# Two transformer blocks, 256 tokens: dilated attention regrouped by pairs of heads, with values stationary

## What is computed

```python
def banded_window_attention(q, k, v, steps):      # per residue class of a group
    ...
    scores = jnp.where(valid, einsum(q, k) * HEAD_DIM ** -0.5, -inf)
    m = jnp.max(scores, axis=-1, keepdims=True)
    p = jnp.exp(scores - m)
    den = jnp.sum(p, axis=-1, keepdims=True)
    out = einsum(p / den, v)
    lse = m + jnp.log(den)

# DILATED_GROUPS = ((128, 1), (512, 4), (2048, 16)), 4 heads of 64 in each
alpha = jax.nn.softmax(jnp.stack(lses, axis=-1), axis=-1)
mixed = jnp.einsum('bshg,bshgd->bshd', alpha, o_all)
```

## Time and profile before

| | |
|---|---|
| Median of three runs | 707.49 us (707.36 to 707.54) |
| The profiled execution | 708.1 us |
| Its span, first to last instruction | 706.3 us |
| Busy: PE / weight loads / DVE / ACT | 697.0 / 615.3 / 492.2 / 400.1 us |
| Mean granted TensorE clock | 0.998 |
| HBM read | 122.36 MB, 175 GB/s over the span |

### The profile page before, as it was taken

How to read it: one execution, slowest core, us unless ns; L and a number is a source line. 1 busy time by engine, 2 the same in 40 slices (tenths; PEclk the granted TensorE clock), 3 DMA queues, 4 the chain that set the end, 5 groups by cost and what they waited for, 6 DMA issues and landing times.

```text
span 706.3 us, 10194 instructions
## 1 busy us (share of the span) xinstructions
PE 697.0 (99%) x4200; PEld 615.3 (87%) x4200; DVE 492.2 (70%) x669; ACT 400.1 (57%) x496; POOL 9.4 (1%) x25
## 2 busy tenths in 40 slices
PE   8999999999999999999999999999999999999996
PEld 7789999888888888888888998899988888888885
DVE  5875676979887766666545377677779878886452
ACT  6875855655555554555555555565547666664341
POOL 1000000003000000000000000000000000000000
PEclk9999999999999999999999999999999999999999
DMA  8863324655565555546551335454555545554511
GB/s 315 314 239 120 120 69 171 216 181 194 190 210 179 179 188 196 211 142 218 179 176 63 120 128 193 158 186 173 179 187 201 186 177 182 189 195 169 214 60 59
DMA packets 19341, 124.06 MB, mean 176 GB/s; under 512 B 2272, under 2 KB 2656, under 8 KB 5088
## 3 DMA queue, kind: packets, MB, share of 16 engines
q1 hardware_dynamic: 18144, 120.20, 48.1%
q10 hardware_dynamic: 1152, 3.22, 1.3%
HBM read 122.36 MB, written 1.05 MB: 175 GB/s over the span
## 4 chain that ended last, share of the span: by engine, by line
PE 89%; DVE 3%; ACT 3%; issue 2%; DMA 1%; SPq 1%; DVEq 0%; ACTq 0%
PE psum L1538 33%; PE psum L1539 17%; PE psum L1531 11%; PE psum L1533 11%; PE psum L1532 11%; PE psum L1527 2%; ACT whi L506 2%; DVE wlo L942 1%; DMA raw<-in_stream 1%; PE psum L1987 1%; PE psum L1950 1%; SPq L412 1%; PE psum L1949 0%; PE psum L2020 0%; DVE gates L1450 0%
## 5 line engine op out<-in xcount | busy, mean ns | idle before, releaser
L942 DVE TENSOR_TENSOR wlo<-raw,whi 128x2048 fp32r<-128x2048 f32 x110 | 251.8, 2291 | 92.6 <-ACT whi L506 92.6
L506 ACT CAST whi<-raw 128x2048 fp32r<-128x2048 f32 x110 | 209.5, 1907 | 49.8 <-PE psum L1533 44.1
L1538 PE MATMUL psum<-hx,whi 128*128 128x512 f32 x480 | 167.4, 393 | 0.0
L1539 PE MATMUL psum<-hx,wlo 128*128 128x256 f32 x480 | 134.4, 280 | 0.0
L1538 PE MATMUL psum<-yx,whi 128*128 128x512 f32 x352 | 125.3, 400 | 0.4 <-DVE yx L953 0.4
L1538 PEld LDWEIGHTS psum<-hx,whi 128*128 128x128 f32 x480 | 89.8, 187 | 19.8
L1539 PE MATMUL psum<-yx,wlo 128*128 128x256 f32 x352 | 98.8, 281 | 0.0
L1539 PEld LDWEIGHTS psum<-hx,wlo 128*128 128x128 f32 x480 | 90.7, 189 | 0.0
L1538 PEld LDWEIGHTS psum<-yx,whi 128*128 128x128 f32 x352 | 66.1, 188 | 16.9 <-DVE yx L953 0.9
L1539 PEld LDWEIGHTS psum<-yx,wlo 128*128 128x128 f32 x352 | 66.5, 189 | 0.0
L1531 PE MATMUL psum<-whi,hx 128*128 128x512 f32 (+1 forms) x160 | 62.5, 390 | 0.9 <-DVE wlo L948 0.7
(11 more groups left out here) (266 smaller groups left out, 1117.4 us busy)
## 6 DMA issues: line engine op xcount, KB each, us to landing
raw<-in_stream SPq DMA_DIRECT2D x110, 1024.0 KB, 4.8
raw<-in_stream SPq DMA_DIRECT2D x8, 256.0 KB, 6.0
relb<-in_relb ACTq DMA_DIRECT2D x1, 1536.0 KB, 7.8
x<-in_xT SPq DMA_DIRECT2D x4, 256.0 KB, 5.7
raw<-in_stream SPq DMA_DIRECT2D x2, 512.0 KB, 8.2
out_t<-sq SPq DMA_DIRECT2D x2, 320.0 KB, 2.7
final_gain<-in_final_gain ACTq DMA_DIRECT2D x1, 512.0 KB, 3.5
bsp<-in_bsp ACTq DMA_DIRECT2D x1, 384.0 KB, 3.3
```

The source lines that it names most:

```text
L506: act.copy(whi[s][:], raw[s][:]).then_inc(unit_hi, 1)
L942: dve.tensor_tensor(wlo[s][:], raw[s][:], whi[s][:], ALU.subtract).then_inc(unit_lo, 1)
L1538: pe.matmul(bank[b][:], stat[0], mov, start=first, stop=False, skip_group_check=True)
L1539: return pe.matmul(bank[b][:, 0:T], stat[1], mov[:, 0, :], start=False, stop=last, skip_group_check=True)
```

## The change

Scores are made by group instead of by head: `scores2(g)` does all four heads of group g, inside units 3, 5 and 7, each right after the group's q and k are transposed. The heads of a pair alternate. DVE adds the masks of group g (`max2(g)`) into a larger S2 that holds all heads; after the third group it takes the maxima. ACT exponentiates two heads each at units 8 and 9, DVE scales the probabilities by the reciprocal sums (`norm2`), PE turns 18 blocks per pair of heads after units 9 and 10 into banks 2 to 6, ACT copies them at units 10 and 11, and after units 10 and 11 PE multiplies with V stationary (64 columns) and the probabilities streaming. The result is feature-major, its halves are made from bank 7, and O2 and its transposes are gone. gate0, gate1 and gu2 become "f" units. `stats` issues a single matmul for n of 1 and above, and DVE adds the last tile. Buffers and banks are laid out anew (mask_sb, mi, mj, PT2, rtmp move).

```diff
-JOBS2 += [(f"gate{j}", "n" if j < 2 else "f", (19 + j if j < 4 else 11 + j,)) for j in range(8)]
-JOBS2 += [(f"gu{j}", "f" if j < 2 else "n", (j,)) for j in range(3)]
+JOBS2 += [(f"gate{j}", "f", (19 + j if j < 4 else 11 + j,)) for j in range(8)]
+JOBS2 += [(f"gu{j}", "f", (j,)) for j in range(3)]
...
-BANKS2.update({"gate0": (0,), "gate1": (1,), "gu2": (0,)})
-BANKS2.update({name: ((0, 1), (3, 7))[i % 2] for i, name in enumerate(n for n, kind, _ in JOBS2 if kind == "f")})
-WB_BANKS = (2, 3, 1, 0)
+BANKS2.update({name: ((0, 1), (2, 3))[i % 2] for i, name in enumerate(n for n, kind, _ in JOBS2 if kind == "f")})
+WB_BANKS = (2, 3, 0, 1)
...
+for _g in range(NG):
+    for _h in range(HG):
+        PLAN[4 + _h].append(("s2", _g, _h))
+for _r in range(HG // 2):
+    for _i in range(PT_BANKS):
+        PLAN[2 + _i].append(("pt2", _r, _i))
+    PLAN[7].append(("o2", _r))
...
-        S2 = sb("S2", [P, NG, 3 * P], scope=sa)
-        PT2 = sb("PT2", [P, NG, 3 * P], scope=sa)
+        S2 = sb("S2", [P, HG, NG, 3 * P], scope=sa)
...
+            def exp2(h):
+                if h == 0:
+                    act.wait_ge(s2_max, 1)
+                for t in range(TT):
+                    c = slice(0, P) if t == 0 else slice(P, 3 * P)
+                    ins = act.activation(S2[:, h, :, c], S2[:, h, :, c], ACT.Exp, bias=small[:, 64 + 2 * h + t:65 + 2 * h + t],
+                                         accum_out=small[:, 80 + 2 * h + t:81 + 2 * h + t])
+                ins.then_inc(s2_exp, 1)
+
+            def evac_pt2(r):
+
+                if r:
+                    full(act, 7, ("o2", 0))
+                for i in range(PT_BANKS):
+                    w = min(4 * P, (PT_BLOCKS - 4 * i) * P)
+                    full(act, 2 + i, ("pt2", r, i))
+                    act.copy(PT2[:, 4 * P * i:4 * P * i + w], bank[2 + i][:, 0:w]).then_inc(psum_free[2 + i], 1)
+
+            def yb_high(r):
+                full(act, 7, ("o2", r))
+                act.copy(yh[:, 6 + r, :], bank[7][:, r * T:(r + 1) * T]).then_inc(yb_hi, 1)

...
+                if n in (11, 12):
+                    yb_high(n - 11)
...
+                if n in (8, 9):
+                    exp2(2 * n - 16)
+                    exp2(2 * n - 15)
+                if n in (10, 11):
+                    evac_pt2(n - 10)
...
+                    if n == 22:
+                        u_gelu(0)
+                        u_gelu(1)
                     side_half(name, 1)
...
-                dve.tensor_tensor(sq[:, 0:2, :], sq[:, 0:2, :], sq[:, 4:6, :], ALU.add).then_inc(folded, 1)
+                ins = dve.tensor_tensor(sq[:, 0:2, :], sq[:, 0:2, :], sq[:, 4:6, :], ALU.add)
+                if n == 0:
+                    ins.then_inc(folded, 1)
+                else:
+                    done(ins)
+                    dve.tensor_tensor(sq[:, 0, :], sq[:, 0, :], sq[:, 1, :], ALU.add).then_inc(folded, 1)
...
-                if f == KT - 2:
+                if f == KT - 1:
...
+                    if f == KT - 1:
+                        gather(squares0, f)
...
+            def max2(g):
+
+                if g == 0:
+                    dve.wait_ge(masks2_done, 1)
+                for h in range(HG):
+                    full(dve, 4 + h, ("s2", g, h))
+                    for t in range(TT):
+                        c, m = slice(0, P) if t == 0 else slice(P, 3 * P), 6 * h + 3 * t + g
+                        ins = dve.tensor_tensor_reduce(S2[:, h, g, c], bank[4 + h][:, c], mask2[:, g, c], 1.0, -3e38,
+                                                       ALU.add, ALU.max, small[:, m:m + 1])
+                    ins.then_inc(psum_free[4 + h], 1)
+                if g == NG - 1:
+                    for h in range(HG):
+                        freed(dve, 4 + h, ("s2", g, h))
+                    dve.tensor_reduce(small[:, 64:64 + 2 * HG],
+                                      small[:, 0:2 * HG * NG].rearrange("p (q g) -> p q g", g=NG), AX.X, ALU.max,
+                                      negate=True).then_inc(s2_max, 1)
+
...
+            def norm2(r):
+
+                dve.wait_ge(s2_exp, 2 * r + 2)
+                d = small[:, 80 + 4 * r:84 + 4 * r]
+                done(dve.reciprocal(d, d))
+                for h in (2 * r, 2 * r + 1):
                     for t in range(TT):
                         c = slice(0, P) if t == 0 else slice(P, 3 * P)
-                        ins = dve.tensor_tensor_reduce(S2[:, g, c], bank[4 + g][:, c], mask2[:, g, c], 1.0, -3e38,
-                                                       ALU.add, ALU.max, small[:, 3 * t + g:3 * t + g + 1])
-                    ins.then_inc(psum_free[4 + g], 1)
-                for g in range(NG):
-                    freed(dve, 4 + g, ("s2", h, g))
-                dve.tensor_reduce(small[:, 64 + 2 * h:66 + 2 * h],
-                                  small[:, 0:3 * TT].rearrange("p (t g) -> p t g", t=TT), AX.X, ALU.max, negate=True)\
-                   .then_inc(s2_max, 1)
+                        ins = dve.tensor_scalar(S2[:, h, :, c], S2[:, h, :, c], small[:, 80 + 2 * h + t:81 + 2 * h + t], None,
+                                                ALU.mult)
+                    ins.then_inc(p2_normed, 1)
+
+            def yb_low(r):
+                dve.wait_ge(yb_hi, r + 1)
+                dve.tensor_tensor(yl[:, 6 + r, :], bank[7][:, r * T:(r + 1) * T], yh[:, 6 + r, :], ALU.subtract)\
+                   .then_inc(psum_free[7], 1)

...
+                if n in (11, 12):
+                    yb_low(n - 11)
...
+                if n in (9, 10):
+                    norm2(n - 9)
                 split(U_IN2 + n + 2)
+                if n in (3, 5, 7):
+                    max2((n - 3) // 2)
...
+            gather(16, KT - 1)
...
-                b, last = STATS_BANK[n], 1 if n < 2 else KT - 1
+                b = STATS_BANK[n]
                 free(pe, b, ("stats", n))
                 pe.wait_ge(folded, n + 1)
-                pe.matmul(bank[b][:, 0:T], ones[:], sq[:, 0, :], start=True, stop=False)
-                pe.wait_ge(squares, (4, 8, 16, 24)[n])
-                pe.matmul(bank[b][:, 0:T], ones[:], sq[:, last, :], start=False, stop=True).then_inc(psum_full[b], 1)
+                tiles_ = (0, 1) if n == 0 else (0,)
+                for i in tiles_:
+                    ins = pe.matmul(bank[b][:, 0:T], ones[:], sq[:, i, :], start=i == 0, stop=i == tiles_[-1])
+                ins.then_inc(psum_full[b], 1)

             def turn_b(j):
...
+                if u - U_IN2 in (3, 5, 7):
+                    scores2((u - U_IN2 - 3) // 2)
...
+            def turn_p2(r):
+
+                pe.wait_ge(p2_normed, 2 * r + 2)
+                for i in range(PT_BLOCKS):
+                    b, h, g, j = 2 + i // 4, 2 * r + i // 9, i % 9 // 3, i % 3
+                    if i % 4 == 0:
+                        free(pe, b, ("pt2", r, i // 4))
+                    ins = transpose(bank[b][:, i % 4 * P:(i % 4 + 1) * P], S2[:, h, g, j * P:(j + 1) * P])
+                    if i % 4 == 3 or i == PT_BLOCKS - 1:
+                        ins.then_inc(psum_full[b], 1)
+
+            def scores2(g):
+
+                freed(pe, 2, ("tq", g))
+                freed(pe, 3, ("tk", g))
+                for r in range(HG // 2):
+                    for t in range(TT):
+                        for h in (2 * r, 2 * r + 1):
+                            rows, b = slice(HD * (h % 2), HD * (h % 2) + HD), 4 + h
+                            if t == 0:
+                                free(pe, b, ("s2", g, h))
+                                pe.matmul(bank[b][:, 0:P], qT2[rows, g, r, 0:P], kT2[rows, g, r, 0:P], start=True, stop=True)
+                            else:
+                                pe.matmul(bank[b][:, P:3 * P], qT2[rows, g, r, P:T], kT2[rows, g, r, :], start=True,
+                                          stop=True).then_inc(psum_full[b], 1)
+
+            def values2(r):
+
+                for i in range(PT_BANKS):
+                    freed(pe, 2 + i, ("pt2", r, i))
+                free(pe, 7, ("o2", r))
                 for g in range(NG):
-                    if h == 0:
-                        freed(pe, 2, ("tq", g))
-                        freed(pe, 3, ("tk", g))
-                    free(pe, 4 + g, ("s2", h, g))
-                    pe.matmul(bank[4 + g][:, 0:P], qT2[rows, g, r, 0:P], kT2[rows, g, r, 0:P], start=True, stop=True)
-                    pe.matmul(bank[4 + g][:, P:3 * P], qT2[rows, g, r, P:T], kT2[rows, g, r, :], start=True,
-                              stop=True).then_inc(psum_full[4 + g], 1)
-
+                    for s in range(TT):
+                        for i in range(2):
+                            h, rows, at = 2 * r + i, slice(HD * i, HD * (i + 1)), (9 * i + 3 * g + 2 * s) * P
+                            ins = pe.matmul(bank[7][rows, r * T + s * P:(r + 1) * T], v2[:, s, g * UF + h * HD:g * UF + (h + 1) * HD],
```

(9 more changed lines are left out.)

138 lines of the change are left out of this document (22 added, 116 removed).

## The result

The changed kernel takes 699.18 us (median of four runs, 698.63 to 699.51) beside 707.51 for the kernel before on the same chip (707.36 to 708.19): ratio 0.988, 95% interval 0.9863 to 0.9897. On another chip, later, it was 699.24 (698.78 to 699.84) beside 708.54: 0.9873, 0.9858 to 0.9887. The forecast was 698.0, a ratio of 0.9866, with a range of 694.9 to 701.9, which holds both medians. The profiled execution took 698.63 us, its span is 696.7. Of the experiment "One ones-matmul, in the kernel before" two of eleven executions took 854.18 (the profiled one) and 980.53 us, at mean granted clocks of 0.753 and 0.655; they are left out of its ratio, and no row is read from that profile.

The account below looks back on a forecast made before the run. PE's queue was taken to set the time. Gains of 8.1 (attention), 1.3 (square sums) and 0.6 (units), less losses of 0.1 and 0.4, made 9.5: 707.5 - 9.5 = 698.0 us, range 694.9 to 701.9.

Parts of the forecast that it names:

- Scores, 5.1: Attention scores on PE: alternating heads overlap in different row halves, 1.7 us per group, 5.1 for three; gain 4.3.
- Values, 4.6: Probabilities times V on PE: two heads' passes run together, 2.3 us per pair of heads, twice 4.6; gain 3.2.
- the rival without overlap: Values on PE: the two heads' passes don't run together, +3.9 us, 701.9 in total; chance 0.07.
- Attention in all, 8.1: Scores, transposes and values in PE's queue: 21.8 us before, 13.7 after, a gain of 8.1.
- Square sums, 1.3: Three of four normalisations drop one of two ones-matmuls, 0.43 us each: gain 1.3, DVE's added sum hidden in the first two.
- Three units, 0.6: gate0, gate1, gu2: steps of 512 and 256 columns replace three of 256, 0.347 us for 0.360; gain 0.6, side work hidden.
- Loss at the start of FF2, 0.1: Last normalisation: DVE closes the addition with a wait ahead of the low half PE stands at; loss 0.1 us.
- (a): Scores in mid-unit wait for ACT's kT copy: nothing if the copy keeps its place, bound 0.1 us each.
- (b): Exponentials need all three groups; DVE's scalings end 9.3 us after unit 7, PE needs them at 10.9: slack 1.6.
- (c): ACT's copies of v and vg free bank 0 late for PE's unit 10: loss 0.4 us, between 0 and 1.5.
- rival (D): 18 transposes in a row beside thin passes drop the granted clock to 1.2 GHz; slower than before; chance 0.02.
- The cadence: Pairs of 512 and 256 columns keep 0.347 or 0.353 us in FF1 and FF2; left unchanged, 2.1 us either side.

Follow-up runs that it names:

- One ones-matmul, in the kernel before: Kernel before, with the second fold of square sums on VectorE and one ones-matmul instead of two at the three later statistics: 707.29 us beside 708.08, ratio 0.9987.
- mending: Changed kernel with VectorE's making of the second block's normalisation columns ahead of its bf16 split instead of behind it: 698.73 us, ratio 0.9866.

## Why the prediction was right, step by step

*What bounds the kernel.* Right: every saving that reached the time was one in PE's stream.

*Scores, 5.1.* Measured 3 x 1.71 = 5.1. The rows of the first block were the right ones to take the price from, and the alternation is what makes it.

*Transposes, 4.0.* Measured 2.06 for the first turn with entering and leaving, 1.94 for the second, which follows the values directly.

*Values, 4.6.* Measured 2 x 2.30, with 24 passes in 2.10. The reading of the gating's rows (eight double passes and two changes of shape) gave the figure to a tenth, by some luck: the passes took 2.10 for 2.0 forecast, the changes of shape 0.20 for 0.35. The price set for the rival without overlap, 8.5 in all, was too high, since in line a pair's passes took 3.45. The rule that was weighed against it, the Trainium skill's "TensorE: Matmul & The Clock Gate", Part 3 ("The mechanism"), that a weight load overlaps only where its row group differs, is not borne out: all these loads use all rows, and the 24 passes take 0.0875 us each with their loads. The Trainium skill's "TensorEngine Tiling (Array Packing)", "Key Properties", has it that different tiles can load and multiply in parallel; there the trace agrees (2.10 us with neighbours in different column halves, 3.45 without).

*Transposing O, 0.4.* The four transposes took 0.36 (416.48 to 416.84) and some 0.1 around them. The prediction counted them as time alone; the pairs behind them ran at the quick pace, and without them those of gate3 to gate5 are 0.3 slower.

*Attention in all, 8.1.* From the first turn of q and k to the gating PE's time fell by 8.26 (107.65 to 99.39). The gates' part of that is -0.3 and +0.2, so attention itself gave 8.35, some 0.3 more than forecast.

*Square sums, 1.3.* The matmuls went (0.43 three times), the gain did not all follow: one 0.43 came back as the wait at unit 2 (0.47 there for 0.07 before). The step that failed is "in the first two of them PE asks for it a unit or more later, so it is hidden". That was said of DVE's added sum and was true of it; what it left out is the next reader down the chain, ACT's copy of unit 0, which PE met with 0.07 us of delay already in the kernel before (its step there is 0.30 instead of 0.23). The last part gained twice what was forecast, 0.43 and another 0.4 by the pace.

*Three units, 0.6.* Mis-sized: the two gates gave 0.2 instead of 0.4, and gu2's 0.2 was taken back at FF2's start, so that the time shows next to nothing. The step that failed there is "beside units of 5.5 us", which put gu2's side copies and sums at nothing: they delay the chain to FF2's input by 0.3. The price of the new form had been read in FF1, at 0.347, though the prediction itself says that the pair has two cadences and FF2 shows the other.

*Loss at the start of FF2, 0.1.* The waits there grew by 0.37 (from 0.80 to 1.17 beyond the steps). 0.3 of this is the first wait, which gu2's form made. What the named mechanism is worth is the rest: the second wait grew by less than 0.1, and with the additions as before the stretch from the gating on is 0.05 shorter.

*(a)* No wait, as forecast. *(b)* The scalings end at 369.85, the turn starts at 371.16: 1.3 of room for 1.6 forecast, and scaling twice turned it into a wait. *(c)* Didn't come. ACT's and DVE's timelines of the changed kernel:

```profile
367.67 2.18 DVE L1385 TENSOR_SCALAR S<-S,small 128x384 f32<-128x384 f32 x4
...
364.27 0.62 ACT L824 ACTIVATE S<-S,small 128x384 f32<-128x384 f32 x1
...
372.18 0.46 ACT L883 ACTIVATE v<-psum,rcol 128x256 f32<-128x256 f32 x1
372.53 0.46 ACT L884 ACTIVATE vg<-psum,rcol 128x256 f32<-128x256 f32 x1
```

A head takes ACT 1.53 (364.27 to 367.32 for two, where the next cast starts) and not 1.63, and a copy 0.36. The copies are through the bank at 372.99 and PE wants it at 373.14. It was a loss of 0.4 put on a difference of two sums of some 13 us; the sign was not in reach.

*The clock, rival (D).* The granted clock was 1.00, the upper level of 2.4 GHz, through both turns and both blocks of values (start to end of a stretch, PE busy, then the clock behind the engines):

```profile
368.00:372.00 4.00, 4.00 (x23) 3.40 (x22) 4.00 (x5) 4.00 (x8) 0.00 (x0) 1.00 0.37 156
...
378.00:384.00 6.00, 6.00 (x51) 4.83 (x50) 1.24 (x2) 3.03 (x4) 0.00 (x0) 1.00 0.48 175
```

From 388 to 392 it was 1.00 too. Values and transposes followed each other for 4.0 us (378.76 to 382.80) with no dip. The Trainium skill's rule behind this rival ("TensorE: Matmul & The Clock Gate", Part 4: transposes don't count as activity) is not seen at work in these rows; no run here shows more.

*The cadence* was left as it was, with 2.1 us on either side. It flipped in three places: in FF2 for 23 us, which gave 0.4, in gate3 to gate5, which cost 0.3, and in the 16 pairs ahead of the fourth statistics, which cost 0.1. That these nearly cancel is luck. Besides, it was 0.353 in the two new gates, where the sum had 0.347.

*The bounds.* Two figures don't come out of their terms: 698.0 - 2.1 is 695.9, not 695.3, and less the 0.4 of (c) it is 695.5, not 694.9. (By its own terms the sum with exposed loads is 700.5, not 700.4.) Nothing hangs on either.

Where the 1.0 us of the attention stretch went, then: 0.4 at unit 2 (shown by undoing and by mending, which gave 0.5 and 0.6), 0.2 by the pace of the two new gate units (read in the trace, and found again when they were made narrow), 0.3 by the pace of gate3 to gate5 (read in the traces), 0.3 at FF2's start by gu2's form (shown by undoing it) and 0.1 by the pace behind that wait; less the 0.3 that attention gave beyond its forecast.

## What to carry to other kernels

When work is taken out of the engine that sets the time, look one unit further on for the reader it nearly met before: here a delay of 0.07 us in the old trace is where the saving stopped. Work added to an engine with room (gu2's sums on DVE, 71% busy) costs time where a chain to PE runs through it. Matmuls with 64 rows or 64 stationary columns should alternate between the two halves; one changed loop order cost 2.2 and 2.8 us here. And before moving an operation out of the way of an awaited one, see whether it fills a wait: then it costs nothing where it is.

## What the runs showed of the hardware

The alternating pair of a 512-column and a 256-column matmul has two paces, 0.347 and 0.353 us, at the same granted clock (1.00) and with the same operands, and keeps one until something else is issued or PE waits. In FF2 one ones-matmul ahead led to the quick one and two led to the slow one, in all thirteen profiles read here; four transposes ended the quick one wherever they stood (525, 537 and 581 us; sixteen in the first of these). Neither is a rule: in FF1 two ones-matmuls led to the quick one as well, and in the kernel before four transposes (at 416.48) ended a slow one. The spatial gating ended a slow one too (0.353 from 410.09, 0.347 from 430.00 on). Behind the second wait of FF2's start the same instructions ran 16 pairs at 0.347 in some kernels (the kernel before, the one with scores at the unit's end) and at 0.353 in others (the changed one). What inside PE fixes the pace is not known; no run tried it.

Two heads' scores in different row halves take 0.77 us together, one head's alone 0.76 (scores without the alternation).

24 passes with 64 stationary columns take 2.10 us when neighbours lie in different column halves and 3.45 us when they don't.
